# An expert-gate matrix built by an adding scatter into DRAM instead of one-hot products

## The reference, cut to what matters

```
v1, i1 = lax.top_k(s1, PEER_TOPK)
v2, i2 = lax.top_k(s2, PEER_TOPK)
cand = (v1[..., :, None] + v2[..., None, :])      # 16 x 16 sums
vals, pos = lax.top_k(cand, PEER_TOPK)
ids = jnp.take_along_axis(cidx, pos, axis=-1)     # cidx = i1 * 128 + i2
gates = jax.nn.softmax(vals, axis=-1)
h = jnp.einsum('td,tkd->tk', xb, ug)              # ug = u_tab[ids]
a = gelu(h) * gates
out = jnp.einsum('tk,tkd->td', a, vg)             # vg = v_tab[ids]
```

## Time and profile before

| | us |
|---|---|
| median of 3 runs | 2413.36 (2413.35 to 2413.64) |
| profiled execution, its own time | 2416.51 |
| its span | 2414.8 |
| PE busy in the span | 2307.8 |
| DVE busy | 1538.1 |
| ACT busy | 1028.5 |
| POOL busy | 72.5 |
| HBM traffic, mean | 176 GB/s |
| granted TensorE clock, mean | 0.982 |

### The profile page before, as it was taken

One profiled execution on the slowest core, in us unless ns is written; L12 is line 12 of the kernel. 1 busy time (PEld: TensorE's weight loads), 2 busy tenths in 40 slices (PEclk: granted clock), 3 DMA queues, 4 the chain that ended last, 5 costly groups with the idle time before them and its releaser, 6 DMA issues.

```text
span 2414.8 us, 45807 instructions
## 1 busy us (share of the span) xinstructions
PE 2307.8 (96%) x15504; PEld 2135.9 (88%) x15504; DVE 1538.1 (64%) x2726; ACT 1028.5 (43%) x1390; POOL 72.5 (3%) x64
## 2 busy tenths in 40 slices
PE   4999999899899989999999999999999999999996
PEld 4999999897699879999999999999788888888885
DVE  4446655565653568777779898989555555555556
ACT  2444455554444443444443333333444444444442
POOL 0000000000010040000000000000000000000000
PEclk9999999999999999999999999999999999999998
DMA  6655555455544555555554445444566666666663
GB/s 178 189 182 164 172 178 168 155 181 177 192 142 156 187 166 172 182 182 182 181 177 131 160 157 159 157 157 157 182 193 194 202 205 201 201 202 202 206 193 123
DMA packets 116576, 425.28 MB, mean 176 GB/s; under 512 B 13840, under 2 KB 13856, under 8 KB 115520
## 3 DMA queue, kind: packets, MB, share of 16 engines
q1 hardware_dynamic: 112608, 412.14, 54.1%
q0 software_dynamic: 3936, 12.71, 2.2%
HBM read 418.50 MB, written 6.29 MB: 176 GB/s over the span
## 4 chain that ended last, share of the span: by engine, by line
PE 90%; DVE 5%; DMA 3%; issue 1%; ACT 1%; DVEq 0%; SPq 0%; ACTq 0%
PE ps L1212 24%; PE ps L1199 17%; PE ps L1194 17%; PE ps L1195 17%; PE ps L1219 12%; PE ps L1448 2%; DMA raw<-in_w_in 2%; DVE w_lo L720 1%; DMA ln_gb<-in_ln_in 1%; DVE bn L733 0%; DVE x L739 0%; DVE tk_ab L1022 0%; PE ps L1320 0%; PE ps L1390 0%; DVE x L745 0%
## 5 line engine op out<-in xcount | busy, mean ns | idle before, releaser
L720 DVE TENSOR_TENSOR w_lo<-raw,w_hi 128x1024 fp32r<-128x1024 f32 x774 | 957.7, 1239 | 713.7 <-PE ps L1219 418.0
L436 ACT ACTIVATE w_hi<-raw 128x1024 fp32r<-128x1024 f32 x774 | 820.5, 1061 | 1061.2 <-DMA raw<-in_peer_v 384.2
L1194 PE MATMUL ps<-x_t_hi,w_hi 128*128 128x256 f32 x3328 | 835.9, 289 | 21.0 <-ACT v_t L486 12.5
L1195 PE MATMUL ps<-x_t_lo,w_hi 128*128 128x256 f32 x3328 | 820.9, 284 | 0.0
L1194 PEld LDWEIGHTS ps<-x_t_hi,w_hi 128*128 128x128 f32 x3328 | 641.7, 193 | 25.9 <-ACT w_hi L436 15.9
L1195 PEld LDWEIGHTS ps<-x_t_lo,w_hi 128*128 128x128 f32 x3328 | 642.4, 193 | 0.0
L1199 PE MATMUL ps<-x_t_hi,w_lo 128*128 128x256 f32 x3328 | 472.1, 285 | 13.5 <-DVE w_lo L720 13.5
L1199 PEld LDWEIGHTS ps<-x_t_hi,w_lo 128*128 128x128 f32 x3328 | 433.3, 194 | 14.8 <-DVE w_lo L720 14.7
L1212 PE MATMUL ps<-w_hi,x_t_hi 128*128 128x512 f32 x1024 | 315.8, 390 | 3.0 <-DVE x_t_lo L1131 3.0
L1212 PE MATMUL ps<-w_hi,x_t_lo 128*128 128x512 f32 x1024 | 316.1, 390 | 0.0
L1219 PE MATMUL ps<-w_lo,x_t_hi 128*128 128x512 f32 x1024 | 274.1, 389 | 0.0
(11 more groups left out here) (204 smaller groups left out, 1313.8 us busy)
## 6 DMA issues: line engine op xcount, KB each, us to landing
raw<-in_u SPq DMA_DIRECT2D x256, 512.0 KB, 4.6
raw<-in_peer_v SPq DMA_DIRECT2D x256, 512.0 KB, 4.9
raw<-in_w_in SPq DMA_DIRECT2D x128, 512.0 KB, 4.6
raw<-in_branch SPq DMA_DIRECT2D x32, 512.0 KB, 3.9
raw<-in_wout SPq DMA_DIRECT2D x32, 512.0 KB, 3.7
raw<-in_wq SPq DMA_DIRECT2D x32, 512.0 KB, 3.8
raw<-in_pleg SPq DMA_DIRECT2D x32, 512.0 KB, 3.8
x<-in_x SPq DMA_DIRECT2D x2, 1024.0 KB, 6.2
```

The lines of the kernel that those rows point to most:

```text
L436: nc.scalar.activation(HI[:, u % 4, :], RAW[:, u % 4, :], ACT.Copy).then_inc(hi_ready, 1)
L720: v.tensor_tensor(LO[:, u % 2, :], RAW[:, u % 4, :], HI[:, u % 4, :].bitcast(F32), ALU.subtract) \
L1194: mm(o, w(HI, u % 4)[:, k, :], xh[:, ks * half + k, :], start=(s and k == 0), stop=False)
L1195: mm(o, w(HI, u % 4)[:, k, :], xl[:, ks * half + k, :], start=False, stop=False)
```

## The change

The gate matrix is made in DRAM. Two arrays `gates_dram` (one for each tile of 128 tokens, 128 x 128 x 128 floats) are filled with zeros by 16 DMAs of 1 MB from POOL (each 128 partitions x 16 runs of 512 bytes) after unit 16; DVE's first `pool_sums` waits for all of them, since the zeros' source tile shares its place in SBUF with what follows. The top-k handles both tiles together, in 16 steps (`tk0` to `tk15`) for a head and 128 in all. The steps are put one to a unit from unit 7 of wq through pleg to unit 70 of u. Its last step computes for each pick the address of its cell, in `cell_ids`. Gates are made in three batches of heads (0 to 2, 3 to 4, 5 to 7), each with its own exponential on ACT, and are final at units 6, 40 and 82 of u. POOL then issues 256 indirect DMAs, one for each tile and pick rank: 128 cells, one for each token, to each of which the token's gate is added (`compute_op=ALU.add`). Each head's 16 for a tile wait for the tile's previous head to have landed. After the last one POOL reads the matrix back in 128 chunks of two 64 KB DMAs, into three slots `gate_chunks`; DVE multiplies each chunk of `experts` by its slot (`gated`), from unit 151 of u on, five chunks to four units. All 128 chunks of u now run as those of the first half did. The one-hots, their products, the transposes of the picks and the two memsets are gone. On DVE the stages wq, pleg and u are written out without loops.

```diff
-            pool.wait_ge(spill_out, 32)
-            nc.gpsimd.memset(BUF[:, TOPK_CHUNKS:FIRST_ONES, :], 1.0).then_inc(ones_ready, 1)
-            pool.wait_ge(picks_sb, 1)
-            nc.gpsimd.memset(BUF[:, FIRST_ONES:NK, :], 1.0).then_inc(ones_ready, 1)
+            pool.wait_ge(zero_out, 16 * 16)
+            for b, (h0, h1) in enumerate(BATCHES):
+                pool.wait_ge(gates_ready, b + 1)
+                for h in range(h0, h1):
+                    for tt in range(NT):
+                        if h:
+                            pool.wait_ge(scattered[tt], 16 * TOPK * h)
+                        for p in range(TOPK * h, TOPK * (h + 1)):
+                            pool.indirect_dma_start(out=cells[tt], out_offset=bass.IndirectOffsetOnAxis(
+                                ap=ID[:, tt, p:p + 1], axis=0), in_=GATE[:, tt, p:p + 1], in_offset=None,
+                                compute_op=ALU.add).then_inc(scattered[tt], 16)
+            for tt in range(NT):
+                pool.wait_ge(scattered[tt], 16 * PICKS)
+            for k in range(NK):
+                if k >= G_SLOTS:
+                    pool.wait_ge(g_mult, k - G_SLOTS + 1)
+                for tt in range(NT):
+                    pool.dma_start(GR[:, k % G_SLOTS, tt * P:(tt + 1) * P], gates_dram[tt][k]
+                                   ).then_inc(g_in[k % G_SLOTS], 16)
...
+            pool.wait_ge(zero_ready, 1)
+            pool.wait_ge(unit_done, BASE["qk"])
+            for n in range(16):
+                pool.dma_start(gates_dram[n // 8][n % 8 * 16:n % 8 * 16 + 16].rearrange("k p e -> p k e"), ZERO[:, :, :]
+                               ).then_inc(zero_out, 16)
...
+            def tk12(h):
+                ch.link(v.tensor_tensor(EQ[:, :, :, :].rearrange("p a r k -> p (a r) k"),
...
+            def gated(k):
+
+                dve.wait_ge(act_evac, 80 + k + 1)
+                dve.wait_ge(g_in[k % G_SLOTS], 16 * NT * (k // G_SLOTS + 1))
+                v.tensor_tensor(BUF[:, k, :], BUF[:, k, :], GR[:, k % G_SLOTS, :], ALU.mult).then_inc(g_mult, 1)
+
+            st = stage("pleg", KD + 2, gt_block, AH, AL)
+            for n in range(32):
+                conv(None, 4, BASE["wq"] + n + DVE_LEAD)
+                search(n - 7)
+            for n in range(32):
+                if n % 2 == 0:
+                    st(None, n // 2)
+                conv(None, 4, BASE["pleg"] + n + DVE_LEAD)
+                search(25 + n)
+            done = 0
+            for n in range(2 * NK):
+                conv(None, 4, BASE["u"] + n + DVE_LEAD)
+                search(57 + n)
+                for b, at_unit in enumerate((6, 40, 82)):
+                    if n == at_unit:
+                        gates_out(b)
+                while done < min((n - G_FROM) * 5 // 4, n // 2 - 2):
+                    gated(done)
+                    done += 1
+            for k in range(done, NK):
+                gated(k)
```

More of the change, by code:

```diff
@@ L50 @@
 DVE_LEAD = 1
-TOPK_CHUNKS = 64
-FIRST_ONES = 104
+PICKS = HEADS * TOPK
+BATCHES = ((0, 3), (3, 5), (5, 8))
+STAGES = 16
+ROUND = 1.5 * 2.0 ** 23
+G_SLOTS = 3
+G_FROM = 150
 def t5_buckets():
@@ L207, in hybrid_block_kernel @@
         spill = nc.dram_tensor("residual_dram", [NT, P, D], F32, kind="Internal").ap()
+        gates_dram = [nc.dram_tensor(f"gates_dram{tt}", [NK, P, P], F32, kind="Internal").ap() for tt in range(NT)]
         raw_in = [sem(f"raw_in{s}") for s in range(4)]
@@ L966, in _ @@
             xt_lo(1)
-            run("wq", 8, 4, {})
-            run("pleg", 8, 4, {}, pre=stage("pleg", KD + 2, gt_block, AH, AL))
             def settle():
@@ L974, in settle @@
                 v.memset(PAD[:, :], 0.0)
[L976 to L981 removed]
+            each = [(tt, f) for tt in range(NT) for f in range(2)]
+            flat = lambda t, tt: t[:, tt, :, :].rearrange("p a b -> p (a b)")
@@ new lines, in _, with tk0, tk1 @@
+            scores = lambda h, tt, f: SC[:, 2 * h + tt, f, :]
+            first = lambda h: slice(TOPK * h, TOPK * h + 8)
+            second = lambda h: slice(TOPK * h + 8, TOPK * (h + 1))
+            def tk0(h):
+                dve.wait_ge(peer_sb, h + 1)
+                for tt, f in each:
+                    ch.tag(v.max(V16[:, tt, f, 0:8], scores(h, tt, f)))
+                settle()
+            def tk1(h):
+                for tt, f in each:
+                    ch.tag(v.max_index(IU[:, tt, f, 0:8], V16[:, tt, f, 0:8], scores(h, tt, f)))
@@ L995, in tk2, with tk6, tk7, tk8 @@
+            def tk6(h):
+                for tt in range(NT):
+                    ch.tag(v.max(GATE[:, tt, first(h)], flat(CAND, tt)))
                 settle()
-                for f in range(2):
-                    ch.tag(v.max_index(IU[:, f, 8:16], V16[:, f, 8:16], S12[:, f, :]))
+            def tk7(h):
+                for tt in range(NT):
+                    ch.tag(v.max_index(POS[:, tt, 0:8], GATE[:, tt, first(h)], flat(CAND, tt)))
+            def tk8(h):
+                for tt in range(NT):
+                    ch.tag(v.match_replace(flat(CAND2, tt), GATE[:, tt, first(h)], flat(CAND, tt), LOWEST))
@@ L1101, in _ @@
-            dve.wait_ge(act_evac, 80 + TOPK_CHUNKS)
-            onehots(None, 0)
-            onehots(None, 1)
-            conv(None, 4, ub + 3)
-            onehots(None, 2)
-            spread(None, 0)
-            conv(None, 4, ub + 4)
-            onehots(None, 3)
-            onehots(None, 4)
-            spread(None, 1)
-            def u_body(i, last):
-                for j in range(4):
-                    if not (last and j == 3):
-                        onehots(i, j + 1)
-                    conv(i, 4, ub + j + DVE_LEAD)
-                    if j % 2:
-                        spread(i, j // 2)
@@ new lines, in gates_out @@
+            def gates_out(b):
+                h0, h1 = BATCHES[b]
+                dve.wait_ge(ge_exp, b + 1)
+                for tt in range(NT):
+                    g = GATE[:, tt, TOPK * h0:TOPK * h1].rearrange("p (h r) -> p h r", r=TOPK)
+                    total = GSUM[:, 8 * tt + h0:8 * tt + h1]
+                    ch.link(v.tensor_reduce(total, g, AX.X, ALU.add))
+                    ch.link(v.reciprocal(total, total))
+                    ins = v.tensor_tensor(g, g, total.unsqueeze(2).to_broadcast([P, h1 - h0, TOPK]), ALU.mult)
+                    if tt == 0:
+                        ch.tag(ins)
+                ins.then_inc(gates_ready, 1)
```

292 lines of the change are left out of this document (108 added, 184 removed).

## The result

The changed kernel takes **2543.23 us** (median of 4 runs, 2542.49 to 2545.83) against 2413.5 us for the kernel before (4 runs in the same session): a ratio of 1.0539, 95% interval 1.0521 to 1.0557. It is 5.4% slower. The forecast of 2354 was wrong, and the time lies above the range too. The profiled execution has a span of 2541.2 us; its granted clock is 0.948 on the mean.

What follows compares the result with a forecast made beforehand. PE was taken to bound the kernel (90% of the chain). The terms -64.7 - 6.5 - 1 + 3 + 2.5 + 5 + 3 = -59 us took 2416.5 us profiled to 2357.5, median 3.1 lower: 2354 us, range 2335 to 2430.

Steps and rivals of the forecast that it cites:

- the price of an indirect issue: POOL's scatter in u: 1.2 us for each of 256 indirect DMAs, ending near 1230 us, hidden.
- The forecast's own point of decision: Scatter from unit 6 of u must end before DVE's first multiply at unit 151: at most 1.6 us an issue.
- Rival B: POOL issues too slowly, above 1.6 us; DVE and PE stand at unit 151; 2533 at 2.3, typically 2431; chance 0.15.
- Rival C: Indirect issues of the scatter hold DVE's splits and top-k steps in u: 2371 to 2429 us; chance 0.13.
- One-hots and memset: Expert stage u: second half without one-hots, products and spreading -64.7 us; removed memset no longer blocking DVE -6.5 us.
- the start of u: POOL's four remaining operations hold up DVE's top-k steps there: between nothing and another 8 us, taken as +2.5 us.
- Top-k in pleg: In pleg a_lo stands behind a top-k step on DVE, and steps over 1.0 us stop PE: +3 us (0 to 6).
- Zeroing: POOL's 16.8 MB of zeros, from unit 16 until the pooling at 200.3 us, exceed free DMA engine time: +5 us.
- Rival D: The zeros before the pooling cost over 235 ns a packet: 2364 to 2454 us, typically 2400; chance 0.10.
- Traffic: Scatter and read-back traffic beside the weight loads, 58 GB/s more on 182: +3 us (0 to 10).
- Rival E: Small additions slow weight loads until PE waits, 0.3 us on 130 units or more: 2390 us and up; chance 0.06.
- The end: End of the expert stage: a 0.4 us multiply replaces the 1.37 us one ahead of the value table: -1 us.

Runs made afterwards that it cites:

- plain_write: Changed kernel with the 256 indirect DMAs writing their gates in place of adding them, so two picks in one cell are not summed: 2345.0 us.
- light_split: Changed kernel with DVE's split making only 8 of 1024 columns of w_lo in units 7 to 152 of u: 2414.2 us, ratio 0.9996.
- late_alo: Changed kernel with gates multiplied in during the value table, and in pleg the next a_lo ahead of DVE's top-k step: 2352.3 us, ratio 0.9744.

## Why the prediction was wrong, point by point

**The step that failed is the price of an indirect issue.** The forecast said that the trace had none, put the ends at 0.54 or 1.10 us and at 2.3, and took 1.2, "nearest the row in which descriptors set the time". Measured is a pitch of 2.39 us over the scatter (609.2 us for 255 steps). While the splits run it is 2.76 on the mean (413.9 us for the first 150 steps) and 2.88 where every issue meets a split; with DVE standing it is 1.85. The forecast's own point of decision, 1.6 us each, fits the runs: a pitch of 1.46 (plain_write) was hidden and 1.85 unheld, or 1.89 in light_split, was not. Rival B's mechanism is what happened, and its formula with the upper end gave 2533; the run took 2543. That this is so near is in part luck: the 2.3 left out the addition and the gap, and was too low for the issues beside splits and too high for the last 105, beside which none ran. What was wrong was the choice between the ends, and the 0.15 for B.

Three things were missing in the 1.2: the addition (an indirect write is 0.96, and with its hold and gap 1.46 on the mean), the 0.30 us gap behind each indirect issue, and the hold. The hold I had named for the upper end, "one that reads indices could wait for a DVE split each time: 1.10 + 1.23 = 2.3"; the run shows it, 1.04 us. The two prices of the earlier trace rows, a read and a write of plain direct DMAs, were carried over to a different kind of operation. The nearest row told nothing of `compute_op`, and the 1.6 that decided was only 0.4 above my value while the open range reached 0.7 beyond the threshold: with ends at 1.1 and 2.3 and no row between them, B's chance should have been near 0.5.

**Rival C had the right contention and the wrong victim.** L740 kept its 1.24 us on the mean in the whole kernel; the index-reading issue waits for DVE, not DVE for it. Taken so, it belonged to B and made it likelier. The Trainium skill (SBUF — State Buffer, "Who interferes with whom") leaves both ways open: who issues first decides who blocks. For an issue that starts first these runs don't bear that out. In plain_write:

```profile
1202.38 0.96 POOL L429 DMA_INDIRECT gates_dram<-gates,cell_ids  x1 [0.31 <-issue]
1202.90 1.23 DVE L740 TENSOR_TENSOR w_lo<-raw,w_hi 128x1024 fp32r<-128x1024 f32 x1 [1.65 <-PE ps L1221]
1203.65 1.31 POOL L429 DMA_INDIRECT gates_dram<-gates,cell_ids  x1 [0.30 <-issue]
```

The first issue starts 0.52 us ahead of the split, and neither is longer. The second starts with 0.48 us of the split to come and is longer by 0.35. So it is throughout: of the issues that start while a split runs (138 in the changed kernel, 128 in plain_write) all but eight are longer by what is left of the split less some 0.12 to 0.13 us, and by nothing where less than that is left.

**The rest of the sum** is what the run without the scatter shows: 2347.8 against 2354.
- One-hots and memset, -64.7 and -6.5, with the start of u, +2.5: together -68.7. In that run the GELUs from first to last take 742.3 us (880.8 to 1623.1) against 812.2: -69.9. Right.
- The start of u: DVE is blocked by POOL's operations as told. Two splits take 2.99 and 4.65 us, L1057 and L1059 4.57 and 4.37. 254 units at 2.877 are 730.8, so 11.5 us are lost. The forecast's sum had 16.7 - 6.5 + 2.5 = 12.7, while its start of unit 151 was worked out with 10.
- Top-k in pleg, +3: right in mechanism, as late_alo shows. In the window 281 records in 70 us are 2.99 us a unit, which would be +0.19 x 32 = 6. Over the whole stage, from DVE's first split of pleg to its first of u, it is less: 95.6 us before, 98.5 in the changed kernel (+2.9), 100.0 without the scatter (+4.4), and 93.7 in late_alo.
- Zeroing, +5: nothing. PE is busy for 105.00 of 105 us there, and the first pooling sums come at 200.5 (before 200.3). Rival D fell. Its packets took some 180 ns (44.9% of 16 x 105 us for 4144 packets of 4 KB), near the lower end that I had from the output's writes (165). The upper end was misread in part: the 1071 packets of the bias table's write are 535 of 4 KB, at 577 ns each, and 536 of a few bytes, and not 2 KB packets. That the doubled mean, 584, is the right price is luck.
- Traffic, +3: nothing. PE is full in 910 to 1310. Rival E fell. The additions' packets of four bytes took 15.5% of the DMA engines' time in 1100 to 1200 us, and the loads still landed in 4.8 us (before 4.7).
- The end, -1: -1.6 (722.0 against 723.6 us). Right.

The rates of read-back and gating held too: 128 chunks in 300.3 us after the stop.

**What the profile was to show** included the mean of POOL's scatter rows, under 1.6, and the multiply's idle time without a DMA. Both came out against the forecast (2.08 us; 213.5 us), and its last sentence had named the first as the place where the sum would fail.

## What to carry to other kernels

When a plan hangs on hundreds of operations of a kind that no row shows, work out the price at which it fails, and if the bounds lie on both sides of it, give the two outcomes like chances, or measure one such operation first: the threshold here was right and of no use without the price. In these runs the cost of a small GpSimd DMA rose with an index list and with an addition, and with an index list it also waited for DVE operations that read two SBUF tensors, when one was running as it started. In a kernel whose DVE does such an operation in every unit, that sets the pace. And before making a slow background task faster, look for the last place at which its result can be used: moving the multiply one stage later turned 5.4% slower into 2.4% faster with the same slow scatter.

## What the runs showed of the hardware

- An indirect DMA with addition of 128 four-byte cells: 1.54 us to issue, 0.30 us gap; written instead, 0.96; direct, 0.54. Direct with addition, the first 19 start 0.54 us apart and the rest 0.88, with records of 7 us that overlap.
- An addition is a packet for each cell (128 for a DMA), a write 16 for the same cells. 4933 small packets in 100 us took 15.5% of the DMA engines, 50 ns each, and PE stayed full (loads landed in 4.8 us, before 4.7).
- DVE operations with two SBUF inputs and SBUF-to-SBUF copies hold POOL's index-reading issues; operations with one input in PSUM and reductions don't; direct issues aren't held by the splits. An issue is held only where it starts while the split runs, and then for what is left of the split less 0.12 to 0.13 us (1.04 of 1.16 for an addition, 0.35 of 0.48 for a write). Where the issue starts 0.52 us ahead of the split, neither is longer.
- Such an issue locks on to a periodic DVE operation: of 84 issues that start in 1080 to 1320 us 81 take over 2.4 us, and most come one to a unit of 2.88 us (2.58 and the gap), 0.07 us behind the start of a split.
- Filling DRAM from 128 partitions in 512-byte runs: 4 KB packets of some 180 ns, 341 GB/s with the weight loads together in 95 to 200 us, PE full. POOL's 16 issues came in bursts of seven with pauses of 31 us, landing after up to 32 us (8.6 to 32.0).
- In three kernels whose first 32 indirect DMAs write and whose others add, PE ran at a third of its pace or less for 30 us and more, and DVE, ACT and the loads at half of theirs or less, beginning before the first addition was issued. With writes alone or additions alone this did not happen. The cause is open.
